# A divided layer norm: the first modulated tile's rounding moves ahead of the second tile's bias addition on ACT

## What is computed

```python
def layer_norm(x, g, b):
    mu = jnp.mean(xf, axis=-1, keepdims=True)
    var = jnp.mean(jnp.square(xf - mu), axis=-1, keepdims=True)
    return ((xf - mu) * lax.rsqrt(var + LN_EPS)).astype(x.dtype) * g + b

def modulate(h, shift, scale):
    return h * (1.0 + scale) + shift

h_lat = ffn_sublayer(h_lat, ...)      # ends in layer_norm(ALPHA * h + FFN_RES * gate * y, g, b)
h_ctx = ffn_sublayer(h_ctx, ...)
u_lat = modulate(h_lat, m_lat[3], m_lat[4])
u_ctx = modulate(h_ctx, m_ctx[3], m_ctx[4])
y_lat, y_ctx = neighborhood_attention(u_lat, u_ctx, ...)   # begins with u @ w_qkv
```

## Time and profile before

| | us |
|---|---|
| median of 3 runs | 2835.58 |
| lowest, highest | 2834.14, 2840.73 |
| profiled execution, whole | 2838.29 |
| its span | 2836.6 |
| PE busy | 2601.5 (92%) |
| DVE busy | 1660.6 (59%) |
| ACT busy | 904.2 (32%) |
| mean granted clock of PE | 0.96 |

### The profile page before, as it was taken

The page is one execution under the profiler, slowest core; times in us unless marked ns, Lnnn a source line. Parts: engine busy times, 40 slices in busy tenths (PEclk is TensorE's granted clock), DMA queues, the critical chain, the costliest instruction groups (busy, mean ns, idle before and its releaser), DMA issues. The chain is left out here.

```text
span 2836.6 us, 38822 instructions
## 1 busy us (share of the span) xinstructions
PE 2601.5 (92%) x14538; PEld 1906.5 (67%) x14538; DVE 1660.6 (59%) x2517; ACT 904.2 (32%) x1489; POOL 221.3 (8%) x372
## 2 busy tenths in 40 slices
PE   5999998998999999999998878997988999798988
PEld 3888887665887888887887567995666433566322
DVE  3876786544687778877777555666543232563101
ACT  1222235443422223422225444445333100443100
POOL 0010011321001100011010001000002000000000
PEclk9999999999999999999998988998989999898998
DMA  7666562332256856557654126654104799416997
GB/s 269 189 199 181 166 178 75 75 75 82 80 179 200 243 168 185 149 183 226 191 186 96 45 67 227 178 161 119 46 12 204 335 427 427 133 45 261 420 428 336
DMA packets 428861, 528.02 MB, mean 186 GB/s; under 512 B 29766, under 2 KB 382532, under 8 KB 416292
## 3 DMA queue, kind: packets, MB, share of 16 engines
q1 hardware_dynamic: 393188, 399.71, 41.2%
q0 software_dynamic: 35520, 126.24, 14.2%
HBM read 524.85 MB, written 1.05 MB: 185 GB/s over the span
## 5 line engine op out<-in xcount | busy, mean ns | idle before, releaser
L2093 DVE TENSOR_TENSOR wlo<-raw,whi 128x1024 fp32r<-128x1024 f32 x392 | 477.4, 1225 | 214.2 <-ACT whi L1562 202.7
L1562 ACT ACTIVATE whi<-raw 128x1024 fp32r<-128x1024 f32 x392 | 413.0, 1057 | 522.7 <-PE bank L715 486.4
L713 PE MATMUL bank<-xhi,whi 128*128 128x512 f32 (+1 forms) x1560 | 569.4, 365 | 3.0 <-DVE xlo L2729 3.0
L714 PE MATMUL bank<-xlo,whi 128*128 128x512 f32 (+1 forms) x1560 | 560.9, 360 | 0.0
L715 PE MATMUL bank<-xhi,wlo 128*128 128x512 f32 (+1 forms) x1560 | 560.4, 359 | 0.0
L2132 DVE SCALAR_TENSOR_TENSOR acc<-mod_ring,conds,acc 128x1024 f32<-128x1024 f32 x308 | 381.5, 1281 | 11.5 <-DMA mod_ring<-in_w_ada 4.2
L713 PEld LDWEIGHTS bank<-xhi,whi 128*128 128x128 f32 x1560 | 295.3, 189 | 63.1 <-issue 20.7
L715 PEld LDWEIGHTS bank<-xhi,wlo 128*128 128x128 f32 x1560 | 295.2, 189 | 44.6
L714 PEld LDWEIGHTS bank<-xlo,whi 128*128 128x128 f32 x1560 | 295.5, 189 | 42.9 <-issue 0.7
L713 PE MATMUL bank<-hhi,whi 128*128 128x512 f32 (+1 forms) x764 | 268.7, 352 | 0.3 <-DVE hlo L2309 0.3
L1438 PE MATMUL bank<-experts,gathered 128*64 128x512 f32 (+1 forms) x1024 | 239.7, 623 | 29.1 <-DMA experts<-in_w_up 26.2
(11 more groups left out here) (338 smaller groups left out, 3507.1 us busy)
## 6 DMA issues: line engine op xcount, KB each, us to landing
raw<-in_ffn_w_in SPq DMA_DIRECT2D x176, 512.0 KB, 4.5
mod_ring<-in_w_mod POOLq DMA_DIRECT2D x128, 512.0 KB, 4.7
experts<-in_w_gate SPq DMA_DIRECT2D x32, 2048.0 KB, 21.1
experts<-in_w_up SPq DMA_DIRECT2D x32, 2048.0 KB, 20.7
experts<-in_w_down SPq DMA_DIRECT2D x32, 2048.0 KB, 20.6
mod_ring<-in_w_ada POOLq DMA_DIRECT2D x96, 512.0 KB, 4.8
raw<-in_ffn_w_out SPq DMA_DIRECT2D x64, 384.0 KB, 3.9
raw<-in_ffn_w_out SPq DMA_DIRECT2D x64, 320.0 KB, 3.5
```

The costliest lines, as they stand in the source:

```text
L713: pe.matmul(o, wh, hi[:, k0 + k, cols], start=(first and k == 0), stop=False)
L714: pe.matmul(o, wh, lo[:, k0 + k, cols], start=False, stop=False)
L1562: act.activation(whi[:, slot, :], raw[:, slot, :], ACT.Copy).then_inc(*n.mark("hi_ready"))
L2093: dve.tensor_tensor(wlo[:, slot, :], raw[:, slot, :], whi[:, slot, :].bitcast(F32), ALU.subtract)\
```

## The change

In halves_modulated, ACT's order changes for either half of each of the four stops. The iteration k = 0 now rounds tile 0 directly behind its bias addition, the iteration k = 1 has only its bias addition, and from k = 2 on all is as before. The root of the context half stands behind the iteration k = 2 of the latent half, where it stood behind k = 1. DVE, PE, POOL and SP keep their orders.

```diff
-                        if k:
-                            act.wait_ge(*written[k - 1])
-                            act.activation(xhi[:, k - 1, c], hm[:, k - 1, c], ACT.Copy).then_inc(*n.mark("xhi_ready"))
-                        if (g, k) == (0, 1):
+                        if k == 1:
+                            continue
+                        r = max(k - 1, 0)
+                        act.wait_ge(*written[r])
+                        act.activation(xhi[:, r, c], hm[:, r, c], ACT.Copy).then_inc(*n.mark("xhi_ready"))
+                        if (g, k) == (0, 2):
                             half_root(1)
```

## The result

Over 20 runs of each the median went from 2837.62 to 2844.49 us; the ratio of the changed kernel to the one before is 1.0022 (95% interval 1.0013 to 1.0032), so it is some 6.3 us slower (3.7 to 9.1). The forecast was slower by 2.2 us, 0.08%. The direction was right, the size was about a third of it. A second comparison, of 12 runs beside 29, gave 1.0020 (1.0006 to 1.0035). The chance of 0.87 was on a time within 0.2% of before; 0.22% lies just outside, with an interval (0.13% to 0.32%) that reaches to either side. The range ended at 2844, counted from a before of 2835.6; over the 20 runs before was 2 us higher, and the change at 2844.5 is at that end.

What follows compares the result with a forecast made beforehand. TensorE (PE) was taken as the bound, busy 2601.5 of 2836.6 us. Losses of 0.77, 0.63, 0.42 and 0.42 at four stops, 2.2 us, on a median of 2835.6 gave 2837.8 us, range 2831 to 2844.

Steps and rivals of the forecast that it cites:

- Both waits, and what each hangs on: Latent half, each stop: PE's first tile waits on ACT's rounding, its second on DVE's reciprocal; eight waits, 10.6 us.
- The first tile: Latent half's tile 0: rounding 0.35 us earlier, PE's first wait 1.75 falling to about 1.4 us, by itself ending nothing earlier.
- my lower bound: ACT's step from a bias addition's end to the rounding waiting for it: 0.04 us taken, 0.10 the upper end.
- The second tile: Latent half's tile 1: root 0.98 us later, reciprocal held by it, PE's second tile starting 0.84 us later.
- What a delay of 0.84 is worth: At the four stops: delay inside unmoved low-clock stretches counts half, so 2.2 us in all.
- 0.77 + 0.63 + 0.42 + 0.42 = 2.24: Loss in us at the first to fourth stop, delay inside the low-clock stretches counted half.
- the 3.4 of a delay with nothing refunded: Alternative sum over four stops if low-clock stretches move with the work: 4 x 0.84 = 3.4 us.
- a rival with a chance of 0.10: Clock stays low longer at the stops, each like the fourth's 10.1 us: 10.1 us lost, 2845.7; chance 0.10.
- a sign of being wrong: At the stops: low-clock stretches whose total leaves 27 us by more than 7 would show the forecast wrong.
- The context half: Context half: has cover; last xlo moves to 1153.3, PE comes at 1153.7, a cover of 0.4 us.
- The shorter stretches as a rival: Low-clock stretches at stops 1, 2 and 4 shrink to 3.4 us: 2832.3, chance 0.06; vanishing wholly: 2825.5, chance 0.02.
- the lower sum: Four stops' loss with low-clock stretches not moving with the work: 2.2 us rather than 3.4.

Runs made afterwards that it cites:

- e1: The changed kernel with the context half's root back behind the second bias addition, the early rounding of tile 0 kept; ratio to before 0.9996 (0.9983 to 1.0009).
- e2: The kernel before with only the context half's root moved one tile later, roundings as they were; ratio to before 1.0017 (1.0003 to 1.0031).
- e3: The changed kernel with the context's reciprocal on DVE behind xlo of tile 3 and PE's spreading behind tile 5; ratio to before 0.9983 (0.9971 to 0.9995).
- r1_change: The changed kernel run again, unaltered, in 12 runs; median 2843.1 us, ratio to before 1.0020 (1.0006 to 1.0035).
- e8: The changed kernel with PE making the latent half's tile 0 three times, 12 matmuls more per stop; ratio to before 0.9994 (0.9983 to 1.0005).
- e9: The kernel before with PE making the latent half's tile 0 twice, six matmuls more per stop; ratio to before 0.9978 (0.9966 to 0.9990).
- e6_ctx_delay: The kernel before with one more reciprocal on DVE in the context half, behind xlo of its tile 0; ratio to before 1.0011 (0.9997 to 1.0025).
- e4_delay1: The kernel before with one more reciprocal on DVE behind the context's reciprocal at each stop; ratio to before 1.0009 (0.9998 to 1.0020).

## Why the prediction was off by its size

Point by point, in the order of the prediction:

- *Both waits, and what each hangs on.* Right. The second tile's wait hung on the reciprocal in DVE's order, e1 and e2 assign the loss to the root's new place, and with the reciprocal out of the way (e3) it is gone.
- *The first tile.* 0.63 us from bias addition to rounding, 0.60 of it the addition itself: the step is 0.03, just under my lower bound (0.04 to 0.10). Wait 1.40 as forecast.
- *The second tile.* Root 2.36 us behind the bias addition (2.4 forecast), DVE's wait 1.25 (1.2), PE's gap 2.0 (2.0 to 2.2), waits for xlo 14.2 us (14). Tile 1 starts 0.80 us later against the stop's first root at three stops and 0.59 at the first, where 0.84 was forecast for all. The first stop lost its share one tile on, with the wait of 0.58 ahead of tile 2 shown above.
- *What a delay of 0.84 is worth.* This is the step that failed, and the term of the sum that was mis-sized: 0.77 + 0.63 + 0.42 + 0.42 = 2.24, where the runs lost 6.3 us (3.7 to 9.1), more than even the 3.4 of a delay with nothing refunded. I had taken the low stretches of one profile as given, in length and in place. They are neither. The change run again shows other ones at the same four stops:

```profile
437.50:447.70 10.20, 8.31 (x36) 7.86 (x37) 9.02 (x19) 6.74 (x16) 2.42 (x4) 0.50 0.10 30
748.20:751.60 3.40, 3.40 (x14) 3.17 (x15) 2.83 (x8) 3.22 (x9) 0.00 (x0) 0.50 0.00 0
1140.70:1147.50 6.80, 6.71 (x29) 6.21 (x29) 5.75 (x14) 4.54 (x12) 0.00 (x0) 0.50 0.04 12
1533.20:1536.60 3.40, 3.40 (x16) 3.03 (x14) 2.83 (x8) 3.22 (x8) 0.00 (x0) 0.51 0.00 0
```

In the profile of the change itself the lengths are those of before, but counted from each stop's first root the stretches end 0.9, 1.5, 1.4 and 0.4 us later, so they did not end where they ended. The four groups of products, from the stop's first root to the last product, took 1.19, 1.09, 0.91 and 0.57 us longer there, 3.8 in all; in r1_change they take 1.9 us longer than before, in e2_root_only 3.6. Beside that, the runs were at the low clock for 12 us (8 in the second comparison) longer in their means, which I had kept as a rival with a chance of 0.10 and not as a part of the forecast. That rival came true for the mean over the whole kernel, at about 6 of its 10.1 us, but not in the form that it had, longer stretches at the stops: their total was 27 us before, 27 in the change and 24 in r1_change, none of them the 7 us away that I had named as a sign of being wrong.
- *The context half.* No wait for xlo there in the change. The cover was as computed.
- *The shorter stretches as a rival.* Not in the change as a whole, though r1_change has them at two of its stops; e3, e8 and e9 show that they can be had.

On my using the Trainium skill (TensorE: Matmul & The Clock Gate, Part 1: The HAM clock gate) for the lower sum: its sentences that activity releases the clock and that the monitor runs freely agree with these traces. In e9_filled_before, six matmuls more left three of the four stops without a low stretch. And in the two profiles of the changed kernel the clock falls 10.5, 10.5, 9.8 and 7.9 us behind a stop's first root in one and 8.0, 9.5, 10.4 and 9.8 in the other, though the work ahead of it is the same. What I drew from it, that the stretches would therefore end where they end and refund half, doesn't follow: a stretch that keeps no step with the work can't be counted on to stand where one profile has it.

**What stays open.** Why the runs lost 6.3 us and not the 3.4 that tile 1 is late (the interval begins at 3.7, so little or much may be missing), and where the added low-clock time lies. In the two profiled executions the four stops have stretches of the same lengths: before they are 6.80, 6.75, 3.40 and 10.10 us, and in the change

```profile
440.40:447.20 6.80, 6.28 (x26) 5.83 (x27) 6.05 (x13) 4.11 (x11) 1.94 (x3) 0.50 0.00 1
751.00:757.90 6.90, 6.83 (x29) 6.38 (x30) 5.84 (x14) 4.65 (x12) 0.00 (x0) 0.51 0.09 27
1143.60:1147.10 3.50, 3.50 (x17) 3.05 (x15) 2.87 (x8) 3.32 (x9) 0.00 (x0) 0.51 0.00 0
1532.70:1543.00 10.30, 8.73 (x38) 8.29 (x39) 8.62 (x19) 6.83 (x16) 0.00 (x0) 0.50 0.13 38
```

so the added 24 us of that execution lie elsewhere. Some of them lie ahead of the first stop, where nothing was changed: from 40 to 60 us the clock was 0.83 before and 0.74 after. That part of the 12.0 us between those two executions is scatter. The means of the runs give a total only, and one profile per kernel, or two of the change, can't say how the stops' stretches are spread over executions. The other profiles don't settle it: at the four stops the kernels with the late root have 27, 24 and 34 us at the low clock (the change, r1_change, e2_root_only), the kernel before and e6_ctx_delay, which is as before up to the context half, have 27 each. That the root's new place makes the loss is shown; that all of the loss arose within the stops is not.

## What to carry to other kernels

When an instruction is moved up an in-order queue, follow the one that is pushed down (here the root), to whatever sits next on the engine that waits for it (the reciprocal), and from there to the next tile. A gain ahead of work that is soon out of input again is none. And where TensorE falls to its lower clock at a stop, don't take the low stretches of one profile as fixed and discount a delay by them: here the delay of 3.4 us cost 6.3 (3.7 to 9.1), that of 12 us about 15 (11 to 20), and that of e4_delay1, 4 us, something between nothing and 6. Look at the mean clock of all runs beside their times, and test a filling of the gap on the kernel before as well, or its gain is taken for the loss of the change.

## What the runs showed of the hardware

- In the kernel before PE waited 1.75 us, did six matmuls and waited 0.84 to 1.06 us, and between 0.9 us before the end of that wait and 0.7 us behind it the clock fell to 1.2 GHz, at all four stops, for 3.4 to 10.1 us. With six matmuls more in the second wait (e9_filled_before) the clocks of the four windows went from 0.86, 0.86, 0.93 and 0.79 to 1.00, 1.00, 1.00 and 0.93.
- The low stretch at one stop of one kernel is not fixed: 6.8, 6.9, 3.5 and 10.3 us in one profile of the change, 10.2, 3.4, 6.8 and 3.4 in another.
- How much of the scatter is the clock's differs: the 20 runs of the change spread by 4.6 us (standard deviation) in span and by 1.8 us in span times mean clock, but the 29 runs of before in the last comparison by 4.3 and 3.7.
- ACT passed a wait on its own last write 0.03 us after that instruction's end (434.75 + 0.60 = 435.35, start 435.38).
